# First modulation of layer 0 block by tile of features, with the first weight block outside the ring and x loaded and transposed ahead

## What is computed

```
mod = einsum('...d,de->...e', silu(cond), w_ada[l]) + b_ada[l]     # 6 parts of 1024
sh1, sc1, g1, sh2, sc2, g2 = split(mod, 6)
hn = rmsnorm(x, norm_mix[l]) * (1 + sc1) + sh1
proj = einsum('bld,de->ble', hn, w_in[l])                          # 3840 columns, in 8 blocks
```

## Time and profile before

| | |
|---|---|
| runs | 961.50, 958.46, 961.47 us; median 961.47 |
| profiled execution | 959.29 us, span of its trace 957.5 us |
| busy PE, PEld, DVE, ACT, POOL | 920.8, 499.5, 431.7, 158.7, 63.6 us |
| share of the chain that ended last | PE 82%, DVE 10%, DMA 4%, ACT 3% |
| mean granted TensorE clock | 0.992 |
| moved by DMA | 303.63 MB, mean 317 GB/s |

### The profile page before, as it was taken

The page is one execution under the profiler, slowest core; times in us unless marked ns, Lnnn a source line. Parts: engine busy times, 40 slices in busy tenths (PEclk is TensorE's granted clock), DMA queues, the critical chain, the costliest instruction groups (busy, mean ns, idle before and its releaser), DMA issues.

```text
span 957.5 us, 13394 instructions
## 1 busy us (share of the span) xinstructions
PE 920.8 (96%) x5197; PEld 499.5 (52%) x5197; DVE 431.7 (45%) x780; ACT 158.7 (17%) x408; POOL 63.6 (7%) x96
## 2 busy tenths in 40 slices
PE   5999999999999999999999999999989999999996
PEld 2755565668554444344437556657865444444442
DVE  1385886742523122232145999776252221222222
ACT  2202015320210100010111211442021001000100
POOL 1112230020000000000010224000000000000001
PEclk9899999999999999999999999999999999999999
DMA  9997574675999999999996632510189999999993
GB/s 366 392 370 287 220 266 176 247 277 210 381 420 422 421 421 421 421 422 420 422 421 247 234 110 90 196 75 23 50 338 421 421 421 421 421 421 421 421 420 131
DMA packets 48430, 303.63 MB, mean 317 GB/s; under 512 B 7680, under 2 KB 7696, under 8 KB 14960
## 3 DMA queue, kind: packets, MB, share of 16 engines
q1 hardware_dynamic: 42368, 291.52, 75.0%
q0 software_dynamic: 2960, 8.63, 2.7%
q10 hardware_dynamic: 3040, 2.62, 0.8%
HBM read 300.10 MB, written 2.65 MB: 316 GB/s over the span
## 4 chain that ended last, share of the span: by engine, by line
PE 82%; DVE 10%; DMA 4%; ACT 3%; issue 1%; SPq 0%; DVEq 0%; ACTq 0%
PE ps L427 80%; DMA ring<-in_w_in 3%; PE ps L461 2%; ACT eP L1578 2%; DMA ring<-in_w_ada 1%; DVE rt L1055 1%; DVE fa L1261 1%; DVE sq L1212 1%; DVE stat L1055 1%; DVE xy L1255 1%; DVE eP L1359 1%; DVE eP L1357 0%; DVE hnT L1103 0%; DVE proj L1222 0%; DVE t L1300 0%
## 5 line engine op out<-in xcount | busy, mean ns | idle before, releaser
L427 PE MATMUL ps<-ring,proj 128*64 128x512 f32 x1024 | 226.3, 595 | 1.0 <-ACT proj L1823 1.0
L427 PE MATMUL ps<-ring,hnT 128*128 128x512 f32 (+1 forms) x576 | 202.1, 503 | 2.6 <-issue 0.9
L427 PEld LDWEIGHTS ps<-ring,hnT 128*128 128x128 f32 x576 | 106.4, 190 | 74.8 <-issue 64.7
L427 PEld LDWEIGHTS ps<-ring,proj 128*64 128x64 f32 x1024 | 72.7, 137 | 132.8 <-issue 131.1
L427 PE MATMUL ps<-hnT,ring 128*64 128x128 f32 (+2 forms) x576 | 74.7, 346 | 3.2 <-DMA ring<-in_w_in 2.5
L427 PEld LDWEIGHTS ps<-hnT,ring 128*64 128x64 f32 (+1 forms) x576 | 61.6, 163 | 14.2 <-issue 3.1
L427 PEld LDWEIGHTS ps<-proj,xs 128*128 128x128 f32 x512 | 58.4, 192 | 12.5 <-issue 11.4
L427 PE MATMUL ps<-proj 128*128 128x512 f32 x128 | 61.7, 607 | 0.0
L427 PE MATMUL ps<-proj,xs 128*128 128x128 f32 x512 | 61.4, 278 | 0.1
L1550 DVE COPY proj<-ps 128x512 f32<-128x512 f32 x16 | 11.1, 691 | 108.1 <-PE ps L427 108.1
L427 PE MATMUL ps<-ring,silT 128*32 128x512 f32 x384 | 48.8, 629 | 10.9 <-DVE silT L1071 7.0
(11 more groups left out here) (231 smaller groups left out, 921.0 us busy)
## 6 DMA issues: line engine op xcount, KB each, us to landing
ring<-in_w_gate SPq DMA_DIRECT2D x64, 1024.0 KB, 14.5
ring<-in_w_down SPq DMA_DIRECT2D x64, 1024.0 KB, 16.9
ring<-in_w_ada SPq DMA_DIRECT2D x48, 1024.0 KB, 8.7
ring<-in_w_in SPq DMA_DIRECT2D x28, 1024.0 KB, 8.0
eP<-in_w_up SPq DMA_DIRECT2D x16, 1024.0 KB, 16.1
wT<-in_w_up SPq DMA_DIRECT2D x16, 1024.0 KB, 18.1
fa<-in_w_up SPq DMA_DIRECT2D x16, 1024.0 KB, 17.9
xy<-in_w_up SPq DMA_DIRECT2D x16, 1024.0 KB, 19.4
```

What stands on the lines that cost most here:

```text
L427: ins = nc.tensor.matmul(*a, **k)
```

## The change

- The eight loads `ada_x` hold for one tile of features k all 1024 rows of its 128 columns of sh1 and of sc1 (1 MB; the array is laid out so on the host). `sums_of_feature(k)` is eight matmuls with 256 columns moving, in two rounds over the four row quarters of bank 1. `modulation_of_feature(k)` is two matmuls against a new constant `pick`, into bank 7. DVE and ACT then shift and scale tile k alone, and `feature_of_first_block(k)` adds its product with "f" into banks 2 and 3, which zeros have filled before, all four heads, 256 tokens moving.
- The two loads of "f" go to slots 8 and 9 (`eP`, `wT`), ahead of `ada_x` 1 and 4 (`ROWS_AHEAD`).
- `cond`, x group 0, `begin` and x group 1 are issued by SP ahead of all weights; POOL keeps `mods`. Each half of x has its own semaphore.
- PE starts with 14 matmuls with zeros, then `normalized_group` 0, the sums of feature 0, `normalized_group` 1, and then the eight features. The zeros between the steps and ahead of "f" are gone.
- `ADA_BEHIND` of layer 0 is (0, 0, 8, 3, 3, 2, 3, 2): nothing behind "f" and "q", eight behind "a". The last quarter of "a" comes first, then four of the steps, `diagonal` 0 and 1, and four more.

The diff, cut to what the steps speak of:

```diff
-ADA_BEHIND = ((2, 3, 3, 3, 3, 2, 3, 2), (0, 0, 0, 0, 0, 3, 0, 0))
+ADA_BEHIND = ((0, 0, 8, 3, 3, 2, 3, 2), (0, 0, 0, 0, 0, 3, 0, 0))
+ROWS_AHEAD = (1, 4)
...
+            for name, dst, src in (("cond_dma", condT[:], ap["cond"]), ("x_dma0", x[:, 0], ap["x_prompt"][0]),
+                                   ("begin_dma", C["begin"][:], ap["begin"]), ("x_dma1", x[:, 1], ap["x_sample"][0])):
+                sp.dma_start(dst, src).then_inc(S(name), 16)
...
-                    for step in EARLY:
-                        load_ada(*step)
+                    for k in range(KC):
+                        if k in ROWS_AHEAD:
+                            r = ROWS_AHEAD.index(k)
+                            load_rows(*IN_BLOCKS[0], r, RING + r)
+                        load(flat_slot, ap["ada_x"][k])
...
+                def sums_of_feature(k):
+                    pe.wait_ge(S("bank1_free"), c.claim(1))
+                    s = slot()
+                    for i in range(KC):
+                        q = slice(32 * (i % 4), 32 * (i % 4) + 32)
...
+                def modulation_of_feature(k):
+                    pe.wait_ge(S("bank7_free"), c.claim(7))
+                    pe.wait_ge(c.of("modX", 0, 0, k), c.at("modX", 0, 0, k))
...
+                def feature_of_first_block(k, ss, banks):
+                    for g in range(NG):
+                        pe.wait_ge(c.of(f"hn1S{g}", k), c.at(f"hn1S{g}", k))
...
-                b = next_bank()
-                if not l:
-                    stream_zeros(b, 5)
-                ss = open_block("f")
-                by_head_and_group("f", 0, ss, b)
-                by_head("f", 1, ss)
...
+                    stream_zeros(f_banks[0], 12)
+                    stream_zeros(f_banks[1], 2)
+                    pe.wait_ge(c.of("begin_dma", 0), c.at("begin_dma", 0))
+                    normalized_group("hn1", "xn1", 0, banks=(4, 5))
+                    pe.wait_ge(c.of("silT"), c.at("silT"))
+                    sums_of_feature(0)
+                    normalized_group("hn1", "xn1", 1, banks=(6, 0))
+                    ss = []
+                    for k in range(KC):
+                        modulation_of_feature(k)
+                        if k + 1 in ROWS_AHEAD:
+                            ss.append(slot(RING + len(ss)))
+                        if k + 1 < KC:
+                            sums_of_feature(k + 1)
+                        feature_of_first_block(k, ss, f_banks)
+                        if k % KH == KH - 1:
+                            owed.append(ss[k // KH])
...
+                if not l:
+                    by_token("a", 1, 1, ss, b)
+                    ada_steps(ADA_BEHIND[l][2] // 2)
                 diagonal(0)
                 diagonal(1)
...
-                    modulation_by_feature(0, 0)
                     for k in range(KC):
+                        dve.wait_ge(c.of("modT", 0, 0, k), c.at("modT", 0, 0, k))
...
+                        ts(hnT[:, k, 0:P], hnT[:, k, 0:P], modT[:, 1, k, 0:1], modT[:, 0, k, 0:1], ALU.mult, ALU.add).then_inc(c.makes("hn1S0", k), 1)
```

More of the change, by code:

```diff
@@ L70, in host_constants @@
     at = [(32 * (2 * a + h), g) for h in range(2) for a in range(2) for g in range(NG)]
+    c["pick"] = np.stack([t % 32 == g for g in range(NG)], 1)
     c["pickm"] = np.stack([t == row + g for row, g in at], 1)
@@ L333, in build @@
         ADA = {"x": (0, 1), "g": (2, 5), "y": (3, 4)}
-        EARLY = [(0, "x", k) for k in range(KC)]
         LATER = [[(0, "g", k) for k in range(KC)] + [(0, "y", k) for k in range(KC)] + [(1, "x", k) for k in range(KC)],
@@ L377, in _, with load_rows @@
                 led.where = f"L{l}"
+                def load_rows(name, col, n, r, s=None):
+                    size = P * KH * n
+                    at = D * IN_AT[name] + r * size
+                    load(lambda s: flat_slot(s)[:, 0:KH * n], ap["w_in"][l, at:at + size].rearrange("(p m) -> p m", p=P), s)
                 if l == 0:
-                    for step in EARLY:
-                        load_ada(*step)
+                    for k in range(KC):
[3 more added lines that the diff above has]
+                        load(flat_slot, ap["ada_x"][k])
                 else:
@@ L386, in _ @@
                     for r in range(2):
-                        size = P * KH * n
-                        at = D * IN_AT[name] + r * size
-                        load(lambda s: flat_slot(s)[:, 0:KH * n], ap["w_in"][l, at:at + size].rearrange("(p m) -> p m", p=P))
+                        if l or name != "f":
+                            load_rows(name, col, n, r)
                     for step in itertools.islice(steps, behind):
@@ L482, in claim_for_norm, with normalized_group @@
                 return b
-            def normalized_group(stage, factors, g, ahead=None, first=None):
+            def normalized_group(stage, factors, g, ahead=None, banks=(None, None)):
                 xv = x[:, g].rearrange("p (k q) -> p k q", k=KC)
                 for h in range(2):
-                    b = claim_for_norm() if h or first is None else first
+                    if banks[h] is None:
+                        b = claim_for_norm()
+                    else:
+                        b = banks[h]
+                        pe.wait_ge(S(f"bank{b}_free"), c.claim(b))
                     if not h:
@@ L553, in at_change @@
                         ada_step(*step)
[L555 to L564, removed]
-                    modulation_by_feature(0, 0)
-                else:
+                def sums_of_feature(k):
[3 more added lines that the diff above has]
+                        q = slice(32 * (i % 4), 32 * (i % 4) + 32)
+                        last = mm(ps[q, 1, 0:2 * P], silT[:, i, :], by_k(s, 2 * P)[:, i] if i < KH else flat_slot(s)[:, 2 * P * i:2 * P * (i + 1)], start=i < 4, stop=i >= 4)
+                        if i < KC - 1:
+                            pay(last)
+                    last.then_inc(c.fills(1, "ada", 0, "x", k), 1)
+                    owed.append(s)
@@ new lines, in modulation_of_feature @@
+                def modulation_of_feature(k):
+                    pe.wait_ge(S("bank7_free"), c.claim(7))
+                    pe.wait_ge(c.of("modX", 0, 0, k), c.at("modX", 0, 0, k))
+                    for a in range(2):
+                        last = mm(ps[:, 7, NG * a:NG * (a + 1)], modX[:, 2 * P * (k % 2) + P * a:2 * P * (k % 2) + P * (a + 1)], C["pick"], start=True, stop=True)
+                        if not a:
+                            pay(last)
+                    last.then_inc(c.fills(7, "modT", 0, 0, k), 1)
@@ new lines, in feature_of_first_block @@
+                def feature_of_first_block(k, ss, banks):
+                    for g in range(NG):
+                        pe.wait_ge(c.of(f"hn1S{g}", k), c.at(f"hn1S{g}", k))
+                    for p in range(2):
+                        for hl in range(2):
+                            for d in range(2):
+                                col = 64 * (2 * p + hl) + 256 * d
+                                last = mm(ps[64 * d:64 * d + 64, banks[p], 256 * hl:256 * (hl + 1)], by_k(ss[k // KH], 512)[:, k % KH, col:col + 64], hnT[:, k, :], start=False, stop=(k == KC - 1), skip_group_check=True)
+                                if k == KC - 1 and hl and d:
+                                    last.then_inc(c.fills(banks[p], "projP", "f", p), 1)
+                                else:
+                                    pay(last)
@@ L567, in _ @@
+                if l:
                     normalized_group("hn1", "xn1", 0, at_change)
                 def wait_for_input(g, half):
-                    label = ("hn1S", g, half) if l else (f"hn1S{g}", half)
-                    pe.wait_ge(c.of(*label), c.at(*label))
+                    pe.wait_ge(c.of("hn1S", g, half), c.at("hn1S", g, half))
                 turn_of_banks = itertools.cycle((2, 3, 0))
@@ L598, in by_head_and_group @@
                     for g in range(NG):
-                        if l and g:
+                        if g:
                             normalized_group("hn1", "xn1", 1)
@@ L786, in ada_behind @@
                     ada_steps(ADA_BEHIND[l]["fqabirvs".index(name)])
-                b = next_bank()
-                if not l:
-                    stream_zeros(b, 5)
-                ss = open_block("f")
-                by_head_and_group("f", 0, ss, b)
-                by_head("f", 1, ss)
+                if l:
+                    b = next_bank()
+                    ss = open_block("f")
+                    by_head_and_group("f", 0, ss, b)
+                    by_head("f", 1, ss)
+                else:
+                    f_banks = [next_bank() for _ in range(2)]
+                    pe.wait_ge(c.of("zero", 0), c.at("zero", 0))
+                    stream_zeros(f_banks[0], 12)
[15 more added lines that the diff above has]
+                            owed.append(ss[k // KH])
                 ada_behind("f")
@@ L1117, in _ @@
```

(28 more changed lines are left out.)

19 lines of the change are left out of this document (11 added, 8 removed).

## The result

The changed kernel takes 976.49 us (975.91 to 977.49, 4 runs) against 960.69 us (958.46 to 961.50, 4 runs) before: ratio 1.0175, 95% interval 1.0152 to 1.0197. It is slower by 15.8 us, outside my range of 948.5 to 957.5 and on the other side. The profiled execution took 977.49 us, its span 975.6 us, 18.1 more than the span before. The prediction also names 976 us, as the time of its slower rival. That is a coincidence: that rival is a clock that falls in the loop, and the clock did not do it.

The account below looks back on a forecast made before the run. Ring loads bound the first 33 us, then TensorE's work. Eight turns of 3.36 us end "f" at 40.7; "b" starts at 73.3, 7.4 us earlier: 951.9 against the profiled 959.29, raised to 952.8 us, range 948.5 to 957.5.

Parts of the forecast that it names:

- slower rival: Loop over features: TensorE's clock falls to half throughout, "f" ends at 66, "b" starts at 96.4, time 976 us; chance 0.06.
- The turn: One feature in block "f"'s loop: modulation 0.49, sums 0.93, visible wait 0.16, "f" 1.78, in all 3.36 us.
- the upper bound: Sums of a feature in the loop: 1.8 us if instructions take 0.111 each without more overlap; 0.93 was taken.
- The lower bound of 0.85: Sums of a feature in the loop: 0.85 us as the array's time, 64-column tiles running two side by side.
- The start: Before the loop's turns: sums of feature 1 start with the third load at 14.04 us, feature 0 done at 16.75.
- x ahead of the weights changes nothing: Load queue at the start: bytes ahead of the tenth load are the same, so x first changes no rail.
- VectorE: Between "f" and "b": its 24.4 us from gates to "hq" end at 65.1, before the diagonals at 65.5.
- "b" at 73.3: Block "b" of layer 0 starts at 73.3 instead of 80.69, 7.4 us earlier, set by its loads.
- My sum of bytes: Loads of "b": shortfall of 1.76 MB, 4.2 us, between 40 and 60 us; a third recovered, between 74.8 and 70.7.
- eaten by the queue: Rival: loads before "b" wait for slots of "a", "b" starts at 78 or later, gain under 2.9, about 959; chance 0.07.
- From there on everything is in the old order: From "b" to the end: order unchanged, loads in hand, so the lead of 7.4 us should stay.
- The forecast of a gain: Whole kernel: 952.8 us, chance 0.55; faster by more than 0.3% in all 0.87.

Follow-up runs that it names:

- The fifth experiment: The first experiment, with block "b" of layer 0 also in slots 8 and 9, ahead of the last two w_ada steps, counters starting at 4: 953.84 us, ratio 0.9945.
- the first experiment: The changed kernel with only the ring's counters starting at 2 instead of 0, so late layer 0 loads fall on their old slots: 958.35 us, ratio 0.9991.
- the third experiment: The changed kernel with two ring slots skipped only at the start of layer 1: 966.72 us, ratio 1.0103.

## Why the prediction was wrong

By its own steps:

- *The turn.* Forecast 3.36 us, measured 3.61. The modulation takes 0.53 us for 0.49 forecast, the wait for the shifted tile, from the end of the modulation to the matmuls of "f", 1.20 for 1.09, and "f" 1.88 for 1.78. The sums, whose rate no row had shown, take their 1.07 us inside that wait, far from the 1.8 of the upper bound. (The lower bound of 0.85 has no row either: half of 0.111 us for each of 16 instructions is 0.89.) Seven turns make 1.8 us.
- *The start.* The third load released the sums at 15.42, forecast 14.04: 1.4 us. I had written that x ahead of the weights changes nothing, but SP now issues four other loads first, and the third load runs from 4.33 us and not from 2.37. No run tests this by itself. In the first feature the clock was at 0.61, 1.35 us more. Together "f" ended at 45.2 and not at 40.7 (43.6 to 44.2 in the experiments, where the clock held).
- *VectorE.* Right: the diagonals do not wait.
- *"b" at 73.3.* Measured 78.5. My sum of bytes assumed that the queue always has a free slot; it ran dry, because SP got the slots of "a" only from 63.6 us on. That is the rival "eaten by the queue", to which I gave 7%, in the place that I had named: "b" at 78 or later, and with the turn set right also its time, 958.4 for "about 959". The fifth experiment, with slots, has "b" at 74.1.
- *"From there on everything is in the old order, the ring has loads in hand ... so the lead should stay to the end."* This is the step that failed, and it decides the sign. The order of the loads is the old one; their slots are not. I took the two loads of "f" out of the ring and counted slots only as far as block "b". It was to be seen: the matmuls of "b" wait for slots 7 and 6 in the order before and 5 and 4 now, and I had set those rows side by side. What the turn costs is some 18 us by the first experiment against the changed kernel, and 22 when put into the kernel before. The fifth experiment shows that a lead can stay to the end as the sentence says: with the turn kept and no half clock at "b", a lead of 6.6 us there is still 5.7 at the end.
- *The slower rival, the clock in the loop.* It did not occur. The granted clock is 0.61 and 0.97 over 16 to 24 us, and 1.00 from there to 44. The rule that I cited from the Trainium skill, page "TensorE: Matmul & The Clock Gate", section "A second HAM failure mode: psum-queue depth-cycling", is stated for bf16 with 512 columns. This float32 loop, which hands over two PSUM banks in every turn, does not bear it out; the gap ahead of "f" is 0.13 us long in a turn. The one fall of the clock, at 16 us, came behind the wait of 1.58 us for the third load.
- *The forecast of a gain.* A gain was there to be had: with the turn set right and slots for "b", the time is 953.8, and 952.8 was my number. But the change as it stands has neither, and a number that fits another kernel is no hit.

## What to carry to other kernels

When loads are taken in turn over a ring and a later stage uses the same buffers by fixed number, the number of loads ahead of that stage, modulo the ring, is part of its schedule: adding or removing a load anywhere before shifts who waits for whom hundreds of microseconds later. After such an edit, compare slot numbers wherever one stage hands the buffers to the next, not only the order.

In these runs a shifted turn cost time only where loads stand close behind those of the stage before. In layer 1 the first expert load comes after 60 + 28 ring loads in the kernel before (slot 0 is next) and 58 + 28 in the changed one (slot 6 is next): layer 1 has eight steps of w_ada, sixteen loads of blocks and four of w_out. So the two kernels differ there by two slots too. Yet SP issues the four loads of w_gate as fast, before and after:

```profile
697.29 1.98 SPq L368 DMA_DIRECT2D ring<-in_w_gate  x4
715.76 2.09 SPq L369 DMA_DIRECT2D ring<-in_w_gate  x4
```

There the queue had been nearly idle for 10 us and more (DMA share 0.01 over 680 to 690 us before, 0.00 over 700 to 710 after), and SP hardly waited for slots. In layer 0 the router's eight steps of w_ada stand right ahead of the experts on the queue.

And a load moved ahead needs a free slot as much as bandwidth: ahead of a stage that waits for loads, look for DMA shares that fall while TensorE is busy.

## What the runs showed of the hardware

The clock of TensorE does not answer in the same way to nearly the same waits. In the loop a wait of 1.58 us behind 0.5 us of nearly empty matmuls was followed by a feature at half clock (3.30 us for 1.95) in the changed kernel; in four other kernels with waits of 1.53 to 1.58 us in the same place the clock stayed at 1.00. Ahead of block "b", waits of 3.23 and 3.33 us in the changed kernel and the first experiment were followed by 5.27 and 5.37 us for the first eight instructions, and a wait of 3.11 us in the third experiment was not:

```profile
76.71 3.67 PE L441 MATMUL ps<-ring,hnT 128*128 128x512 f32 x8 [3.11 <-issue]
```

In layer 1, behind a wait of 2.2 us for VectorE's xs, the clock was 0.83 over 10 us in the profiles of the changed kernel and the first experiment, and 1.00 in those of before and the third. From there to the next wait for xs it is 46.1 us in the first two and 44.8 in the others, so this is worth 1.3 us. So a microsecond or so between two profiles of such a kernel says nothing about an edit.

Over 350 to 435 us, where only the 1 MB loads of the experts run, DMA moved 420 to 421 GB/s at a share of 1.01 in every kernel, and a round of experts that is bound by it takes 29.9 us to within 0.2 us. A full share alone does not mean that rate: over 52 to 56 us the changed kernel has a share of 1.01 and moves 340 GB/s. POOL's loads of small rows fall into that stretch; that they are the cause is not shown.
